# Spreading the inverse roots of the first half of the sequence: eight fp32 products of 128 columns become two rounded products of 512, one column block later

## The reference

```
hn = x * rsqrt(mean(x*x, axis=-1) + 1e-6) * norm_g
a, b, gate = split(hn @ w_in, 3)                # 3 x 1024 columns
u = a * sigmoid(b)
u = causal depthwise convolution of u over 31 taps + conv_b
u = layer_norm(u) * ln_g + ln_b
u = silu(u) * silu(gate)
out = x + u @ w_out
```

## Time and profile before

| | |
|---|---|
| three timed runs | 363.04, 363.13, 363.56 us |
| median | 363.13 us |
| the profiled execution, its own time | 363.72 us |
| its span in the trace | 361.9 us, so 1.82 us lie outside it |
| PE busy | 356.9 us, 99% of the span |
| DVE, ACT, POOL busy | 88%, 64%, 75% |
| granted TensorE clock | 1.00 of full speed throughout, the 2.4 GHz level |

### The profile page before, as it was taken

How to read it: one execution, slowest core, us unless ns; L and a number is a source line. 1 busy time by engine, 2 the same in 40 slices (tenths; PEclk the granted TensorE clock), 3 DMA queues, 4 the chain that set the end, 5 groups by cost and what they waited for, 6 DMA issues and landing times.

```text
span 361.9 us, 4758 instructions
## 1 busy us (share of the span) xinstructions
PE 356.9 (99%) x1564; PEld 289.2 (80%) x1564; DVE 319.9 (88%) x514; ACT 232.4 (64%) x334; POOL 269.8 (75%) x194
## 2 busy tenths in 40 slices
PE   7999999999999999999999999999999999999996
PEld 6888888888888888888888888888888888888885
DVE  4779799999999899999999998993798979997952
ACT  5889685558847772998667875975655951452400
POOL 0029999999999997899999999795796532359220
PEclk9999999999999999999999999999999999999999
DMA  7995011201411311406112214235713695066042
GB/s 260 403 400 206 34 60 58 91 28 58 116 60 53 65 60 58 116 2 116 58 60 51 67 58 80 96 58 103 246 59 117 237 404 173 0 203 205 31 169 92
DMA packets 30520, 43.51 MB, mean 120 GB/s; under 512 B 18336, under 2 KB 18848, under 8 KB 30496
## 3 DMA queue, kind: packets, MB, share of 16 engines
q1 hardware_dynamic: 30352, 43.21, 37.7%
q10 hardware_dynamic: 144, 0.00, 0.0%
HBM read 34.82 MB, written 4.19 MB: 108 GB/s over the span
## 4 chain that ended last, share of the span: by engine, by line
PE 97%; DMA 1%; SPq 0%; ACT 0%; DVE 0%; issue 0%
PE mm L632 68%; PE acc L711 12%; PE mm L711 9%; PE mm L649 6%; DMA raw<-w_in 1%; PE acc L702 0%; PE acc L692 0%; PE acc L626 0%; ACT w_hi L786 0%; DVE nat L1273 0%; SPq L494 0%; SPq L520 0%; PE acc L620 0%; PE acc L622 0%
## 5 line engine op out<-in xcount | busy, mean ns | idle before, releaser
L632 PE MATMUL mm<-x_hi,w_hi 128*128 128x512 f32 x352 | 139.3, 396 | 0.0
L632 PE MATMUL mm<-x_hi,w_lo 128*128 128x512 f32 x352 | 139.0, 395 | 0.0
L632 PE MATMUL mm<-x_lo,w_hi 128*128 128x512 f32 x352 | 139.0, 395 | 0.0
L1185 DVE SCALAR_TENSOR_TENSOR acc<-u,chan,acc 128x512 f32<-128x512 f32 x157 | 110.7, 750 | 0.1
L632 PEld LDWEIGHTS mm<-x_hi,w_lo 128*128 128x128 f32 x352 | 66.1, 188 | 16.0
L632 PEld LDWEIGHTS mm<-x_hi,w_hi 128*128 128x128 f32 x352 | 66.1, 188 | 15.8
L632 PEld LDWEIGHTS mm<-x_lo,w_hi 128*128 128x128 f32 x352 | 66.1, 188 | 15.8
L1494 POOL TENSOR_TENSOR pconv<-pconv,prod 128x512 f32<-128x512 f32 x60 | 77.3, 1312 | 1.3 <-ACT prod L868 1.3
L1185 DVE SCALAR_TENSOR_TENSOR acc<-u,w_sum,acc 128x512 f32<-128x512 f32 x90 | 67.5, 750 | 1.3 <-ACT acc L850 1.1
L868 ACT ACTIVATE prod<-u,chan 128x512 f32<-128x512 f32 x69 | 47.7, 714 | 15.6 <-POOL pconv L1494 14.3
L1438 POOL TENSOR_TENSOR w_lo<-raw,w_hi 128x1024 fp32r<-128x1024 f32 (+1 forms) x21 | 49.7, 2365 | 9.3 <-ACT w_hi L817 9.2
(11 more groups left out here) (109 smaller groups left out, 541.2 us busy)
## 6 DMA issues: line engine op xcount, KB each, us to landing
raw<-w_in SPq DMA_DIRECT2D x22, 512.0 KB, 3.3
nat<-x_t SPq DMA_DIRECT2D x16, 256.0 KB, 6.1
sgate<-x SPq DMA_DIRECT2D x8, 512.0 KB, 10.8
raw<-w_out SPq DMA_DIRECT2D x8, 512.0 KB, 3.3
nat<-x SPq DMA_DIRECT2D x8, 512.0 KB, 7.9
y<-nat SPq DMA_DIRECT2D x15, 256.0 KB, 2.1
raw_late<-w_out SPq DMA_DIRECT2D x4, 512.0 KB, 4.1
sig<-w_out SPq DMA_DIRECT2D x4, 512.0 KB, 3.9
```

Of the source, the lines that this page charges most:

```text
L632: ins = nc.tensor.matmul(bank(("unit", m, h)), w[:, m % 3, k, :], xx[:, k, half(h)], start=(k == 0 and i == 0), stop=(k == KC - 1 and i == 2))
L1185: ins = nc.vector.scalar_tensor_tensor(dst, chain_in(j, chain, k), tap(j, chain, k), chain_bank(j, chain), ALU.mult, ALU.add)
```

## The change

The first half's spread is made as the second half's was. POOL gets a new function, `split_rms`, after each of the two `inverse_rms` of half 0: one operation writes the rounded part of the inverse roots (type fp32r) and one the rest. ACT makes two diagonals of each tile, eight in all, in `diags`, after half 1's spread has read it. PE multiplies them in two matmuls of 512 columns with `ones_r`; the first waits for seven of the eight diagonals, the second for all. The spread stands before column k = 3 of the pass (3, 0) instead of k = 2. The new tensor `rms_parts` takes 32 bytes of each partition, ahead of `stats` and what follows.

```diff
-SPREAD_AT = {1: (0, 4), 0: (3, 0, 2)}
+SPREAD_AT = {1: (0, 4), 0: (3, 0, 3)}
...
         half_neg = sb("half_neg", [P, NT])
+        rms_parts = sb("rms_parts", [P, 2, TPH], F32R)
...
+        rms_parts_ready = sem("rms_parts_ready")
...
-        def diag(i):
-
-            return sgate[:, i, 0:P]
-
...
             def spread_rms(h):
 
+                spread = rms_spread(h).rearrange("p (t q) -> p t q", t=TPH)
+                pe.wait_ge(ones_r_ready, 1)
                 if h == 1:
-                    spread = rms_spread(1).rearrange("p (t q) -> p t q", t=TPH)
-                    pe.wait_ge(ones_r_ready, 1)
                     pe.wait_ge(diag_hi_ready, TPH)
-                    nc.tensor.matmul(spread, ones_r[:], diags[:, 0, :, :], start=True, stop=False)
+                else:
+                    pe.wait_ge(diag_ready, 2 * TPH - 1)
+                nc.tensor.matmul(spread, ones_r[:], diags[:, 0, :, :], start=True, stop=False)
+                if h == 1:
                     pe.wait_ge(diag_lo_ready, TPH)
-                    ins = nc.tensor.matmul(spread, ones_r[:], diags[:, 1, :, :], start=False, stop=True)
                 else:
-                    for i in range(TPH):
-                        pe.wait_ge(diag_ready, i + 1)
-                        ins = nc.tensor.matmul(rms_spread(0)[:, i * P:(i + 1) * P], ones[:], diag(i), start=True, stop=True)
-                ins.then_inc(rms_all_ready, 1)
+                    pe.wait_ge(diag_ready, 2 * TPH)
+                nc.tensor.matmul(spread, ones_r[:], diags[:, 1, :, :], start=False, stop=True).then_inc(rms_all_ready, 1)
...
             def rms_diagonal(t):
 
                 act.wait_ge(ident_in, 16)
-                act.wait_ge(rms_ready, rms_count(t))
-                nc.scalar.activation(diag(t), ident[:], ACT.Copy, scale=rms[:, t:t + 1]).then_inc(diag_ready, 1)
+                act.wait_ge(rms_all_ready, 1)
+                for i in range(2):
+                    act.wait_ge(rms_parts_ready, 2 * (rms_count(t) - TPH - 1) + i + 1)
+                    nc.scalar.activation(diags[:, i, t, :], ident[:], ACT.Copy,
+                                         scale=rms_parts[:, i, t:t + 1].bitcast(F32)).then_inc(diag_ready, 1)
...
+            def split_rms(tiles):
+
+                part = slice(tiles[0], tiles[-1] + 1)
+                done = 2 * (rms_count(tiles[0]) - TPH - 1)
+                pool.wait_ge(rms_ready, rms_count(tiles[0]))
+                nc.gpsimd.tensor_scalar(rms_parts[:, 0, part], rms[:, part], 1.0, 0.0, ALU.mult,
+                                        ALU.add).then_inc(rms_parts_ready, 1)
+                pool.wait_ge(rms_parts_ready, done + 1)
+                nc.gpsimd.tensor_tensor(rms_parts[:, 1, part], rms[:, part], rms_parts[:, 0, part].bitcast(F32),
+                                        ALU.subtract).then_inc(rms_parts_ready, 1)
+
...
             inverse_rms(range(TPH - 1))
+            split_rms(range(TPH - 1))
             inverse_rms((TPH - 1,))
+            split_rms((TPH - 1,))
```

## The result

The changed kernel takes 363.97 us (median of 22 runs) where the kernel before took 363.52 us beside it (22 runs). The ratio is 1.0019, with a 95% interval of 1.0011 to 1.0028: slower by 0.7 us (0.4 to 1.0), where 0.42 us of gain were forecast. The 0.19% lies inside the 0.2% that I had called indistinguishable, but 22 runs on each side tell it from zero, and it has the other sign.

A forecast was written before the change was run, and what follows sets the result against it. PE, busy for 99% of the span, was taken as the bound. Products costing 0.88 us replaced by ones costing 0.46 save 0.42; 363.13 - 0.42 = 362.71 us. Forecast's own range 362.4 to 363.0, with rivals 362.3 to 363.45.

The forecast's parts named there:

- rival (c): Moving all later tensors by 32 bytes matters: 0.36 us either way, giving 362.3 or 363.1 us; chance 0.06.
- the 1.82 us outside the span: Time around the profiled execution's span of 361.9 us, kept unchanged in the sum.
- The removed products: Eight fp32 products of the first half's spread on PE, said to cost 0.88 us.
- the new ones: Two 512-column matmuls replacing them on PE, said to cost 0.46 us as in the other half.
- POOL's first scale: New scale on tiles 0 to 2, held until DVE's two-input operation is through, ending at 34.28.
- ACT's eight diagonals: ACT making eight diagonals for the spread: 2.44 us, from about 34.34 to 36.87.
- The cover at the second product: Diagonals ready at 36.87, PE wanting all eight at 37.70: 0.77 us left after the signal, so no stall.
- the cover at the means: DVE's aggregates 1.5 us before PE's spread of the means at 259.02; at worst 0.5 us left after the change.
- Rival (a): The saving is lost to a wait, for the diagonals or for DVE at 259: 363.1 us; chance 0.14.
- (b): POOL's small operations all slow, PE stalls 0.85 us in the spread: 363.56 us; chance 0.07.
- (d): A rounded product costs as much as four fp32 ones, so PE saves nothing: 363.1 us; chance 0.01.
- the splits of x_lo: Two splits starting at about 41.25 instead of 40.52, wanted by PE at 46.05: 2.2 us and more left.

The follow-up runs named there:

- e1: The kernel before with only the unused 32-byte tensor rms_parts added at its place; 363.86 us, ratio 1.0022.
- h4: The kernel before with 32 bytes of padding behind sig, moving only the first stage's and output stage's tensors; 364.02 us, ratio 1.0023.
- f4: The kernel before with POOL's four new operations and their semaphore, results unused, rms_parts behind diags; 363.75 us, ratio 1.0010.
- g3: The kernel before with four plain fp32 POOL subtractions to an unread tensor, no semaphore or wait; 363.52 us, ratio 1.0010.
- g2: The kernel before with only the first two of POOL's new operations and their semaphore, results unused; 363.57 us, ratio 1.0000.
- e3: The changed kernel with rms_parts behind diags, so all other tensors lie as before; 363.45 us, ratio 1.0002 to the kernel before.
- h1: The changed kernel with rms_parts behind diags, one split of all four tiles, spread before k = 5; 363.25 us, ratio 1.0001 to the kernel before.
- e4: The changed kernel with the first spread of the means one column later; 363.75 us, ratio 1.0016 to the kernel before.
- f3: The changed kernel with rms_parts padded to 64 bytes; 361.39 us, ratio 0.9960 to the kernel before.
- g1: The kernel before with 64 bytes of padding where the changed kernel has its 32-byte tensor; 361.12 us, ratio 0.9944.
- g4: The changed kernel with rms_parts padded to 64 bytes and later spreads of means and deviations; 359.50 us, ratio 0.9892 to the kernel before.
- h2: The changed kernel with 64 bytes, later mean and deviation spreads, one split of four tiles, spread before k = 5; 360.00 us, ratio 0.9909 to the kernel before.
- h3: The kernel before with 64 bytes of padding behind sig, moving only the first stage's and output stage's tensors; 360.18 us, ratio 0.9921.
- i1: The kernel before with 64 bytes of padding and later spreads of means and deviations, nothing of the change; 358.56 us, ratio 0.9868.
- i2: The changed kernel with 64 bytes and later spreads of means and deviations, run again; 359.57 us, ratio 0.9901 to the kernel before.
- f1: The kernel before with 32 bytes of padding only in front of the output stage's weights; 363.66 us, ratio 1.0006.

## Why the prediction was wrong

**The step that failed** is the rival (c) of the prediction, "the 32 bytes that move all later tensors matter", which I gave 0.06. The sum puts it at nothing, on the argument "157 DVE steps whose input starts 4 bytes further with each tap lie within 739 to 764 ns, and PE's rate is the same for tensors in many places". The rows were DVE's, and PE was the engine that sets the time. For PE the second half of the sentence was wrong in the very profile that I had: 66 projection matmuls in 15.34 us are 232.4 ns each, and 948 in 221.19 are 233.3. Two paces with one shape and one clock say that something besides columns and clock enters. I had given "a thousandth of the span, 0.36 us" either way; measured were 0.40 us on PE's path and, over many runs, a ratio of 1.0022 and 1.0023 for those 32 bytes alone (e1, h4), some 0.8 us with 0.4 and 0.5 as the lower ends. So up to half of what the 32 bytes cost stands in no chain above; the faster executions that they seem to take away may be a part of it.

**A second term was missing.** The sum took the 1.82 us outside the span as fixed. POOL's four operations make them 2.14 (f4, g3 against g2). The terms as measured are: products -0.41, place of the tensors +0.40, outside the span +0.33, together +0.32 us, and +0.6 in executions where PE also waits for the means. The measured ratio is +0.7 us with an interval of 0.4 to 1.0; the loss of the faster pace in one run of five would add 0.2. What is left is within the noise and has no term of its own. The absolute forecast, 362.71, was 1.26 us below the measured 363.97; 0.39 of that is its base, since the three runs that I had gave a median of 363.13 and all 22 give 363.52.

**What held.** The removed products cost 0.88 us and the new ones 0.46: PE's distance from half 1's spread to the means fell by 0.41 to 0.42 us in e3 and h1. POOL's first scale was held by DVE's two-input operation (0.67 us, forecast 0.67 from 33.6 to 34.28), the others took 0.19, ACT's eight diagonals 2.46. The Trainium skill (GPSIMD Engine Reference, Specifications) says that such a DVE instruction contends with GpSimd for SBUF; this trace and f4's, 0.67 again, agree.

**What was too generous.** The cover at the second product was 0.77 us by the sum and nothing in the profile, a stall of 0.05; the cover at the means was 0.5 us at worst by the sum, and 0.31 us of wait in the profile. Both margins were worked out within one execution, and the start shifts PE against the others from one to the next, by 0.7 us between these two profiles. The cover at the means also had two errors of its own. It set 259.02, a time of the chain, against 257.51, a time of the timeline, in which the same product starts at 258.85: the lead was 1.34 us, not 1.5. And DVE was not 0.56 but 0.81 us later, by the late transpose and the wait at the merge. In e3, e4 and h1 a lead of 0.5, 0.9 and 0.2 us was left at that place. Rival (a) thus holds in part, in some executions; rivals (b) and (d) don't hold. One more sum was off without a consequence: the pass in which the splits of x_lo are wanted comes 0.42 us earlier too, so they had 1.8 us to spare, not 2.2.

None of the signs of being wrong that I had named came: PE's waits list neither the diagonals nor the means, and the last diagonal ended at 37.28, before 37.6. They watched the covers and not the two terms that failed.

## What to carry to other kernels

When PE bounds a kernel, a new tensor can be an edit of PE's pace: put it where it moves nothing, or run the old kernel with the same number of bytes as padding beside the new one, before a tenth of a per cent is put down to the edit. Trying a few paddings is worth more than such an edit (here 64 bytes gave 0.6 to 0.8%, the edit at most 0.1%). Compare time and span in every run, since time outside the span is in no chain. When two times are compared, take both from the same view.

## What the runs showed of the hardware that was not expected

- The distance between the starts of 512-column fp32r matmuls took four values in stretches with the granted clock at 1.00: 229, 232.4, 233.3 and 234.3 ns. 64 bytes in front of the projection's tensors gave 229 (f3, g1, g4, h2, h3, i1, i2); 32 bytes in front of the output stage's weights gave 234.3 there in place of 233.3 (the changed kernel, e1, e4, f1, h4). Why a start address does this is open: no run moved one operand alone, so it isn't known whether the stationary or the moving one decides.
- The pace of 232.4 ns came over the whole projection in one profile (g3) with the same places as before; so the place doesn't fix the pace alone, and the execution seems to have a part.
- The time outside the span rose by 0.33 us in one step between two and four more GpSimd operations.
- Behind a wait of 2.36 us PE's granted clock was 0.50 for some 3 us in one profile (f3), which cost 1.6 us, and stayed at 1.00 behind a wait of 2.37 us in another (g1).
